# A hybrid mLSTM and attention block: ScalarE's first copies, the split of the squares and the place of the weighting are changed

## What is computed

```python
proj = _rmsnorm(x, pre_g) @ w_in                   # 1024 rows, 1024 -> 11280 columns
m_qk = jax.nn.silu(_centred_dwconv(m_qk, conv_w, conv_b))
...
# mLSTM, both directions, 4 heads, per chunk:
s = jnp.einsum('nhjd,nhsd->nhjs', qb, kb) * jnp.exp(D - mj[..., None])
num = w_inter[..., None] * jnp.einsum('nhjd,nhde->nhje', qb, C) + jnp.einsum('nhjs,nhse->nhje', s, vb)
h = num / jnp.maximum(jnp.abs(den), jnp.exp(-mj))[..., None]
C_new = decay[..., None, None] * C + jnp.einsum('nhs,nhsd,nhse->nhde', wk, kb, vb)
...
# differential attention, 8 heads:
a = softmax(s[:, :, 0]) - lam * softmax(s[:, :, 1])
o = _rmsnorm(a @ v, a_norm_g) * (1.0 - lam_init)
...
y = g_a * (h_a @ w_branch_m) + g_b * (h_b @ w_branch_a)
return x + _rmsnorm(y @ w_out, post_g)
```

## Time and profile before

| | us |
|---|---|
| median of 3 runs | 1600.18 (1599.32 to 1601.27) |
| the profiled execution | 1599.01, its span 1597.2 |
| TensorE busy | 1565.8 (98%) |
| VectorE busy | 909.2 (57%) |
| ScalarE busy | 817.3 (51%) |
| GpSimd busy | 481.0 (30%) |

### The profile page before, as it was taken

The page is one execution under the profiler, slowest core; times in us unless marked ns, Lnnn a source line. Parts: engine busy times, 40 slices in busy tenths (PEclk is TensorE's granted clock), DMA queues, the critical chain, the costliest instruction groups (busy, mean ns, idle before and its releaser), DMA issues.

```text
span 1597.2 us, 23770 instructions
## 1 busy us (share of the span) xinstructions
PE 1565.8 (98%) x8539; PEld 1304.4 (82%) x8539; DVE 909.2 (57%) x1541; ACT 817.3 (51%) x1460; POOL 481.0 (30%) x596
## 2 busy tenths in 40 slices
PE   7899999999999999999999999999999999999998
PEld 5588888888888877788888888888888888888998
DVE  5613675775775737767777767776765003334313
ACT  5224555654655635565656565555564235556312
POOL 4233143252152142222222222222221223433650
PEclk9999999999999999999999999999999999999999
DMA  5031121021221131111111111111111635423322
GB/s 170 17 131 48 33 80 53 26 92 39 62 70 40 32 90 27 40 40 40 40 41 40 40 40 41 40 41 40 42 59 50 198 110 193 144 80 105 121 91 106
DMA packets 139353, 111.47 MB, mean 70 GB/s; under 512 B 7098, under 2 KB 126843, under 8 KB 139268
## 3 DMA queue, kind: packets, MB, share of 16 engines
q1 hardware_dynamic: 134660, 97.77, 21.0%
q10 hardware_dynamic: 4608, 12.58, 2.1%
HBM read 85.14 MB, written 21.00 MB: 66 GB/s over the span
## 4 chain that ended last, share of the span: by engine, by line
PE 92%; DVE 4%; ACT 2%; POOL 1%; DMA 1%; issue 1%; SPq 0%; DVEq 0%; POOLq 0%; ACTq 0%
PE ps L773 62%; PE ps L781 10%; PE ps L982 6%; PE ps L1089 6%; PE ps L995 4%; PE ps L873 1%; PE ps L1022 1%; PE ps L801 1%; PE ps L1004 1%; POOL w_split L651 0%; PE ps L907 0%; DMA raw_a<-qk_f 0%; PE ps L793 0%; DVE h_sum L1395 0%; SPq L529 0%
## 5 line engine op out<-in xcount | busy, mean ns | idle before, releaser
L773 PE MATMUL ps<-xn_split,w_split 128*128 128x512 f32 x4224 | 1023.6, 397 | 7.9 <-ACT v_f L1644 7.9
L773 PEld LDWEIGHTS ps<-xn_split,w_split 128*128 128x128 f32 x4224 | 782.6, 188 | 189.0 <-issue 13.3
L651 POOL TENSOR_TENSOR w_split<-w_raw,w_split 128x256 fp32r<-128x256 f32 x384 | 309.8, 837 | 965.6 <-ACT w_split L1637 965.5
L1927 ACT ACTIVATE probs<-ps,negmax 128x1024 f32<-128x1024 f32 x128 | 142.5, 1114 | 106.7 <-DVE negmax L1458 105.7
L1483 DVE TENSOR_TENSOR aT_split<-ps,aT_split 128x512 fp32r<-128x512 f32 x128 | 88.2, 689 | 130.0 <-ACT aT_split L1932 130.0
L1458 DVE TENSOR_REDUCE negmax<-ps 128x1 f32<-128x1024 f32 x128 | 150.7, 1219 | 16.3 <-PE ps L982 16.3
L1932 ACT ACTIVATE aT_split<-ps 128x512 fp32r<-128x512 f32 x128 | 76.3, 596 | 100.6 <-PE ps L995 94.0
L982 PE MATMUL ps<-ak_split,aq_split 64*128 64x512 f32 x768 | 106.2, 408 | 2.7 <-DVE ak_split L1413 2.7
L781 PEld LDWEIGHTS ps<-aT_split,va_split 128*128 128x128 f32 x768 | 95.8, 189 | 4.6 <-issue 2.6
L1637 ACT ACTIVATE w_split<-w_raw 128x1024 fp32r<-128x1024 f32 x94 | 99.0, 1053 | 0.0
L781 PE MATMUL ps<-aT_split,va_split 128*128 128x256 f32 x768 | 97.7, 284 | 0.0
(11 more groups left out here) (238 smaller groups left out, 1641.0 us busy)
## 6 DMA issues: line engine op xcount, KB each, us to landing
w_raw<-in_w_in SPq DMA_DIRECT2D x80, 512.0 KB, 3.9
qk_f<-spill_g SPq DMA_DIRECT2D x16, 512.0 KB, 3.7
spill_g<-qk_f ACTq DMA_DIRECT2D x12, 512.0 KB, 2.7
w_argument<-m_rows SPq DMA_DIRECT2D x8, 512.0 KB, 4.9
spill_m<-hT_f ACTq DMA_DIRECT2D x16, 256.0 KB, 2.2
spill_a<-o_out SPq DMA_DIRECT2D x32, 128.0 KB, 1.8
h_split<-spill_m SPq DMA_DIRECT2D x8, 512.0 KB, 5.1
w_raw<-in_w_branch_m SPq DMA_DIRECT2D x8, 512.0 KB, 5.8
```

The lines of the kernel that those rows point to most:

```text
L651: lo = pool.tensor_tensor(wsp[b][:, 1, ks_], raw[b][:, ks_], wsp[b][:, 0, ks_].bitcast(F32), ALU.subtract)
L773: mm = pe.matmul(ps[:, half, :], wsp[b][:, wl, k, :], moving[:, xl, k, cols], start=(k == 0 and n == 0), stop=(k == KT - 1 and n == 2))
L1927: act.activation(pr[:, c], ps[:, 2 + 2 * c:4 + 2 * c, :].rearrange("p b k -> p (b k)"), ACT.Exp, bias=nmax[:, b, c:c + 1], accum_out=den[: ...
```

## The change

Three parts of the program change.

1. **Prologue.** On ScalarE, the copies of projection results move to other places among the row exponentials: the second half of tile 1 is read before `exp_f`; tile 2 is read between `ln_f` and `decay`, and between `emj` and `w_k`; `conv_sigmoid(0, 0)` comes after the first half of tile 3. On TensorE the four groups of gate-row transposes stand in tiles 4 and 5 (before: 3 and 4), and the matmul that brings the reversed columns back stands inside tile 6 (before: between tiles 5 and 6).
2. **Squares.** The squares are split like other operands: ScalarE makes a rounded copy, DVE subtracts it, and TensorE does two fp32r matmuls with a rounded matrix of ones. Before, it was one float32 matmul.
3. **mLSTM step.** On DVE, the state's low part and the weighting of the next step's scores stand before the denominator chain.

```diff
@@ TensorE, prologue
-            for half in range(2):
-                proj_half(0, 0, 0, 2, half)
+            for j in range(2, 4):
+                for half in range(2):
+                    proj_half(0, 0, 0, j, half)
...
-            for j in range(3, 5):
-                proj_half(0, 0, 0, j, 0, amid=lambda: gate_columns(2 * j - 6))
-                proj_half(0, 0, 0, j, 1, amid=lambda: gate_columns(2 * j - 5))
-            for half in range(2):
-                proj_half(0, 0, 0, 5, half)
...
+            for j in range(4, 6):
+                proj_half(0, 0, 0, j, 0, amid=lambda: gate_columns(2 * j - 8))
+                proj_half(0, 0, 0, j, 1, amid=lambda: gate_columns(2 * j - 7))
+            proj_half(0, 0, 0, 6, 0, amid=columns_back)
+            proj_half(0, 0, 0, 6, 1)
@@ TensorE, squares
-                pe.wait_ge(a_osq.sem, a_osq.after(h, n))
-                pe.matmul(ps[:, 7, 2 * P:4 * P], ones[:], osq[:], start=True, stop=True).then_inc(a_ss.sem, 1)
+                pe.wait_ge(a_osq_lo.sem, a_osq_lo.after(h, n))
+                for a in range(2):
+                    mm = pe.matmul(ps[:, 7, 2 * P:4 * P], ones_r[:], osq_s[:, a], start=(a == 0), stop=(a == 1))
+                mm.then_inc(a_ss.sem, 1)
@@ VectorE, m_step (the lines that make scores' product are now weigh_scores)
+                if t < NC - 1:
+                    dve.wait_ge(chi_done.sem, chi_done.after(h, t))
+                    dve.tensor_tensor(cs[:, 1], cf[:], cs[:, 0].bitcast(F32), ALU.subtract).then_inc(clo_done.sem, 1)
+                    weigh_scores(h, t + 1)
                 dve.tensor_scalar(dsm[:, 0], num[:, :, MV], -1.0, None, ALU.mult).then_inc(den_chain.sem, 1)
...
-                if t < NC - 1:
-                    dve.wait_ge(chi_done.sem, chi_done.after(h, t))
-                    dve.tensor_tensor(cs[:, 1], cf[:], cs[:, 0].bitcast(F32), ALU.subtract).then_inc(clo_done.sem, 1)
@@ VectorE, attention (a block q; also once after the last head)
+            def o_square_low(h, n):
+                dve.wait_ge(a_osq.sem, a_osq.after(h, 2 * n + 1))
+                dve.tensor_tensor(osq_s[:, 1], osq[:], osq_s[:, 0].bitcast(F32), ALU.subtract).then_inc(a_osq_lo.sem, 1)
...
                     a_low_round(h, q, 0)
+                    if q == 0 and not first:
+                        o_square_low(h - 1, 3)
+                    if q in (2, 4, 6):
+                        o_square_low(h, q // 2 - 1)
@@ ScalarE, prologue
             read_conv_half(0, 0, 0, 0, 0, 1, done=3)
+            read_conv_half(0, 0, 0, 1, 1, 1)
             act.wait_ge(prep_dve, prep_dve_at("abs_f"))
...
+            read_gate(0, 0, 0, 2, 0, 0, gate_fill, bmerge[:, 0:1])
             act.wait_ge(prep_dve, prep_dve_at("decay"))
...
-            read_conv_half(0, 0, 0, 1, 1, 1)
...
+            read_gate(0, 0, 0, 2, 1, 0, gate_fill, bmerge[:, 0:1])
             act.wait_ge(prep_dve, prep_dve_at("w_k"))
             mark(act.activation(r_wk[:], r_wk[:], ACT.Exp), "w_k")
-            read_gate(0, 0, 0, 2, 0, 0, gate_fill, bmerge[:, 0:1])
-            conv_sigmoid(0, 0)
-            read_gate(0, 0, 0, 2, 1, 0, gate_fill, bmerge[:, 0:1])
             for n in range(1, 4):
                 for half in range(2):
                     read_gate(0, 0, 0, 2 + n, half, n, gate_fill, bmerge[:, n:n + 1])
+                    if (n, half) == (1, 0):
+                        conv_sigmoid(0, 0)
@@ ScalarE, o_square
                 act.activation(osq[:], ps[:, 7, 0:2 * P], ACT.Square).then_inc(a_osq.sem, 1)
+                act.wait_ge(a_osq.sem, a_osq.after(h, 2 * n))
+                act.activation(osq_s[:, 0], osq[:], ACT.Copy).then_inc(a_osq.sem, 1)
```

More of the change, by code:

```diff
@@ L854, in gate_columns, with columns_back @@
                     mm.then_inc(prep_pe, 1)
-            for j in range(3, 5):
-                proj_half(0, 0, 0, j, 0, amid=lambda: gate_columns(2 * j - 6))
-                proj_half(0, 0, 0, j, 1, amid=lambda: gate_columns(2 * j - 5))
-            for half in range(2):
-                proj_half(0, 0, 0, 5, half)
-            pe.wait_ge(prep_dve, prep_dve_at("col_rev"))
-            pe.matmul(ps[:, 7, 0:NC * Q_ALL * MH], rev[:], colrev[:].rearrange("p c q m -> p (c q m)"),
-                      start=True, stop=True).then_inc(prep_pe, 1)
-            for half in range(2):
-                proj_half(0, 0, 0, 6, half)
+            def columns_back():
+                pe.wait_ge(prep_dve, prep_dve_at("col_rev"))
+                pe.matmul(ps[:, 7, 0:NC * Q_ALL * MH], rev[:], colrev[:].rearrange("p c q m -> p (c q m)"),
+                          start=True, stop=True).then_inc(prep_pe, 1)
+            for j in range(4, 6):
[3 more added lines that the diff above has]
+            proj_half(0, 0, 0, 6, 1)
             def tr_round(h, k, srcs, first=False):
@@ L1319, in m_step @@
                 dve.tensor_tensor(wt[:], scores, wt[:], ALU.mult).then_inc(ptf_done.sem, 1)
+            def m_step(h, t):
+                if t == 0:
+                    weigh_scores(h, t)
                 if t < NC - 1:
```

11 lines of the change are left out of this document (9 added, 2 removed).

## The result

The changed kernel takes 1583.42 us (median of 4 runs, 1582.7 to 1583.6). The kernel before, timed beside it, takes 1600.36 (1599.32 to 1601.27). The ratio is 0.9893, with a 95% interval of 0.9876 to 0.9911. The profiled execution took 1582.70, its span 1580.7. But several terms of its sum were off, in both directions, and the trace shows which.

The account below looks back on a forecast made before the run. TensorE's row of matmuls plus its gaps was taken to bound the kernel. 9.7 + 6.1 + 1.3 - 1.0 - 0.4 = 15.7 us from the 1600.18 median gave 1584.5 us; range 1581.5 to 1587, to 1590 with two rivals.

Parts of the forecast that it names:

- What bounds the kernel: Whole kernel: TensorE, busy 1565.8 of 1597.2 us; edits count by closing gaps, shortening its row or making another engine late.
- Prologue: Prologue: removing TensorE's 7.86 us gap before 71.44 and 1.8 us of half clock gains 9.7 us.
- the half clock: Prologue, 36 matmuls after the gap: they take 10.45 us where 8.6 would do, costing 1.8 us.
- the 0.3 us of spare at tile 4: Prologue: GpSimd's low part for tile 4 is done at 80.0, when TensorE wants it at 80.3.
- the replay: Prologue: the new order reckoned on paper, with 5.6 us per half tile, exp_f at about 59.65 and DVE's row chain 0.7 late.
- Squares: Attention: two fp32r matmuls replace each float32 square, gaining 0.19 us at each of 32 squares, 6.1 us in all.
- the rival that they are not dearer: Attention squares: a float32 square costs 0.25 against 0.24 us, so nothing is gained, 1590.6 us; chance 0.05.
- Last square: End of attention: TensorE, already waiting 0.47 us for the last square, waits about 1.0 us more.
- Block 2: Attention, block 2 of a head: the subtraction delays the row maxima and nearly uses up the spare; 0.4 us lost in all.
- the rival: Attention, block 2: the subtraction collides with GpSimd's gate product, held 0.5 us each, costing 3 to 4 us: 1588; chance 0.12.
- The slower case: Attention: DVE's chain sets the pace at all blocks following a square, giving about 1615 us; chance 0.02.
- mLSTM step: mLSTM step 7: pt's low part comes some 0.45 us earlier, removing most of four 0.4 us waits; gain 1.3 us.

Follow-up runs that it names:

- the copies late: The changed kernel with all of ScalarE's prologue in the order of before, TensorE's transposes staying late: 1592.73 us, ratio 0.9956.
- the float32 squares alone: The changed kernel with TensorE's square matmuls as before, in float32, while the copy, subtraction and waits are kept: 1587.88 us, ratio 0.9922.
- The doubled subtraction: The changed kernel with each DVE subtraction for the squares made twice, first into a tile nobody reads: 1593.32 us, ratio 0.9959.

## Why the prediction was right, and where its terms were off

**What bounds the kernel: right.** What was gained is either a shorter row of TensorE matmuls or a gap closed: 6.6 us of the 16.5 are busy time, the rest gaps.

**Prologue, 9.7 forecast, 9.17 measured.** Both pieces went: the gap of 7.86, and the half clock. With the GpSimd wait taken away too, the prologue is 95.23 - 85.16 = 10.07 us shorter than before, which puts the half clock and the restart at 2.2 us (1.8 forecast). The table of stretches gives the same: at 0.50 the clock stood for 6.8 us, to about 75.4, and matmuls ran from 71.44, so for 4.0 of them, of which half is lost. The price from the Trainium skill ("TensorE: Matmul & The Clock Gate", Terms), 3.4 us as an estimate, does not agree: taken over all of the 6.8 us, it counts the time at half clock in which no matmul ran. How long the lower level lasts varies from run to run: 10.2 us in the kernels with the step alone and with the copies late, whose prologues took 95.91 and 95.39 us.

The step that failed is the 0.3 us of spare at tile 4: a wait of 0.62 came, worth 0.90. The start of exp_f was as reckoned: 60.05 after, 1.13 later than in the earlier trace rows, of which 0.49 is the later start of the program and 0.64 stands against 0.73 in the replay. But DVE's row chain lost more behind it. The high part for tile 3, which now comes ahead of exp_f, sets GpSimd going beside DVE's scan (GpSimd and DVE of the changed kernel):

```profile
60.29 3.82 POOL L655 TENSOR_TENSOR w_split<-w_raw,w_split 128x256 fp32r<-128x256 f32 x4 [4.80 <-ACT w_split L1660]
...
63.55 2.71 DVE L1250 TENSOR_TENSOR_SCAN row_t<-row_reset,row_f 36x1024 f32<-36x1024 f32 x1
67.63 2.28 DVE L1256 TENSOR_TENSOR_SCAN row_m<-row_carry,row_i 36x1024 f32<-36x1024 f32 x1
```

The first scan here took 2.28 us before, when GpSimd was idle there; the second one, with GpSimd idle again, takes 2.28 in both. (GpSimd's last piece was itself held up by the DVE instruction ahead of the scan; it ended at 64.12, and the scan 2.14 us after it.) Behind the scan the chain is 1.13 us late in place of 0.7. Then GpSimd began 0.35 us later than in the replay and took 5.76 us for tile 4, not 5.42, now with all four pieces beside the convolution. It was done at 81.10, where the replay, moved by the 0.49, had 80.5. TensorE in turn was there earlier than the replay had it, at 80.54 instead of 80.8, since its halves take 5.55 us and not 5.6. The two together, 0.6 and 0.25, turn 0.3 us of spare into the wait of 0.6. The replay did not have the collision in it: durations were taken from before, where these two instructions never met. The text called the place the tightest point and priced the loss at 3 us or more; the truth is 0.9, without a second fall of the clock.

**Squares, 6.1 forecast, about 4.8 measured.** The price of 0.19 was right, and the rival that they are not dearer is refuted (the float32 squares alone make it 4.84 us from the first attention scores to the last). The failed step is the factor of 32. At the squares in block 6, and in head 0, TensorE next waits for DVE, and from four tenths to all of the gain is given back.

**Last square, 1.0 forecast, 0.91 measured**, recorded wait against recorded wait (0.47 to 1.38).

**Block 2, 0.4 forecast, 0 measured.** The subtraction did collide with GpSimd (0.63 us), as the rival had it, but the cover was just enough: the squares in block 2 give their full 0.18 to 0.20. The doubled subtraction shows that nothing is left there: 0.6 to 1.3 us for one more instruction. The rival's mechanism was true and its 3 to 4 us were not, because it took a delay of 0.5 us to exceed what was spare; here the 0.2 us of hindrance did not. The hindrance is what was left of the GpSimd piece that the subtraction met, 0.35 us less 0.14.

**The slower case** did not come. Its condition was no spare at all four places of a head, and the doubled subtraction shows that at blocks 0, 4 and 6 another 0.4 us fits in at next to no cost.

**mLSTM step, 1.3 forecast, 2.66 measured, and about 1.2 more behind it.** The step that failed is the reading of four waits of 0.40 as all there is. Between the pt products of steps 6 and 7, TensorE takes 0.57 to 0.59 us less than before, and 0.08 less in the step after: 0.66 a head. The weight load of the same product was recorded waiting 0.62 us before:

```profile
209.85 0.78 PEld L781 LDWEIGHTS ps<-v_split,pt_split 128*128 128x128 f32 x6 [0.62 <-DVE pt_split L1327]
```

And the sum followed the step only to the end of mLSTM; it did not ask what ScalarE's earlier copies at a head's end set free for attention's start. What they set free there differs from one execution to the next (between nothing and 1.6 us in the ten traces).

**The sum.** 9.17 + 2.66 + 1.23 + 3.84 - 0.49 and 0.1 behind attention make the span's 16.5. The forecast's 15.7 is near it since terms too large by 0.5 and 0.9 met terms too small by 1.4 and 1.2, the last of which was not forecast and is not there in every execution. That closeness is partly luck. The lower end of the range, 1581.5, does not come out of the bounds named for it either: 0.4 for the mLSTM, 0.5 for the squares and 1.2 for the base give 1582.4, still below the measured time.

## What to carry to other kernels

Price an edit on the bounding engine at each place where it acts, and ask what that engine waits for next: where another engine is already level with it, the gain is given back in part, and a weight load's wait may not be in the list at all. Where engines take turns, read what is lost from the starts of neighbouring matmuls, since the wait recorded at the matmul shows only part of it. Where a stretch hangs on a DMA's return, look at more than one trace before giving a gain there a number. When an order is replayed on paper, ask of each instruction that moves what it will newly run beside: DVE and GpSimd lengthen each other, and the trace of before has no row for a pair that never met.

## What the hardware showed that was not expected

- Waits recorded at a matmul understate what their removal gives: 0.40 recorded and 0.66 gained a head, 0.62 and 0.90, 1.38 and 1.68. The difference is each time 0.26 to 0.30 us. The waits of the weight loads at the same three places, 0.62, 1.05 and 1.59 us, come nearer. Why the two rows differ is not shown.
- Two DVE subtractions of 128x256 in a row beside GpSimd took 0.63 and 0.96 us, each ending 0.28 us after the GpSimd piece that it met, and the same instruction took 0.42 in the absence of GpSimd; GpSimd's four pieces grew from 2.82 to 2.99 and 3.18. Beside DVE's convolution, four pieces of 128x256 took 5.4 to 5.8 us of GpSimd's time, where they take 2.83 elsewhere. A scan of 36x1024 took 2.71 beside GpSimd and 2.28 without.
- After a wait of 3.89 us, 24 matmuls took 7.36 instead of 5.78 us, with 3.4 us at a granted clock of 0.50: this gap cost 1.6 us more than itself. The clock also fell, for 3.4 us each, after the waits of 1.84 us (squares alone, before the first attention scores) and 2.25 us (subtraction made twice, last square). After waits of 0.62, 1.38, 1.54, 1.61 and 1.76 us in other kernels it stayed at 1.00.
